# Upper halves of the weights stored with two k-tiles alternating word by word: a two-layer and two-block network on one core

## The reference

```python
def sqrelu_mlp(h, w1, w2):
    return jnp.square(jax.nn.relu(h @ w1)) @ w2
...
        up = jnp.einsum('bsd,df->bsf', h, w_up[l])
        g, val = up[..., :D_FF], up[..., D_FF:]
        g = _causal_dwconv(g, conv_w[l], conv_b[l])
        f = jnp.einsum('bsf,fd->bsd', jax.nn.gelu(g) * val, w_down[l])
        x = _layernorm(DEEPNORM_ALPHA * x + gate2[:, None, :] * f, ln2_g[l], ln2_b[l])
```

## Time and profile before

| | |
|---|---|
| Time, median of 3 runs | 2515.74 us |
| The profiled execution's span, first to last instruction | 2512.5 us |
| Instructions in the trace | 36307 |
| TensorE matmuls busy | 99% of the span, 14058 matmuls |
| Weight loads busy | 85%, 14058 loads |
| VectorE, ScalarE, GpSimd busy | 64%, 39%, 5% |
| HBM traffic | 120 GB/s over the span |

### The profile page before, as it was taken

How to read it: one execution, slowest core, us unless ns; L and a number is a source line. 1 busy time by engine, 2 the same in 40 slices (tenths; PEclk the granted TensorE clock), 3 DMA queues, 4 the chain that set the end, 5 groups by cost and what they waited for, 6 DMA issues and landing times.

```text
span 2512.5 us, 36307 instructions
## 1 busy us (share of the span) xinstructions
PE 2491.2 (99%) x14058; PEld 2125.8 (85%) x14058; DVE 1611.4 (64%) x2551; ACT 972.5 (39%) x1483; POOL 117.9 (5%) x211
## 2 busy tenths in 40 slices
PE   8999999999999999999999999999999999999998
PEld 6888888888888888779888888898888888888887
DVE  5777667665546567766655575776667777644446
ACT  6243533131313245764332244353232454533224
POOL 0000000100000000000000000010001000000000
PEclk9999999999999999999999999999999999999999
DMA  7323314433333321002545553224546323132222
GB/s 288 120 99 110 127 50 143 159 118 110 114 110 134 110 76 51 2 1 93 199 152 169 173 192 113 101 88 172 187 158 219 135 95 110 68 101 93 100 96 97
DMA packets 83965, 303.70 MB, mean 121 GB/s; under 512 B 9200, under 2 KB 11376, under 8 KB 83568
## 3 DMA queue, kind: packets, MB, share of 16 engines
q1 hardware_dynamic: 58336, 208.92, 24.0%
q0 software_dynamic: 25488, 92.81, 10.8%
HBM read 299.60 MB, written 2.10 MB: 120 GB/s over the span
## 4 chain that ended last, share of the span: by engine, by line
PE 96%; DMA 2%; DVE 1%; issue 0%; ACT 0%; SPq 0%; POOL 0%; POOLq 0%; ACTq 0%; DVEq 0%
PE G L648 20%; PE G L650 20%; PE G L649 20%; PE G L675 5%; PE G L676 5%; PE G L677 5%; PE G L742 2%; PE G L743 2%; PE G L744 2%; PE B L1243 2%; PE G L827 1%; DMA Araw<-adaw_dram 1%; PE G L829 1%; PE G L828 1%; PE B L1219 1%; PE G L1203 1%
## 5 line engine op out<-in xcount | busy, mean ns | idle before, releaser
L1391 ACT ACTIVATE Whi<-Wraw 128x1024 fp32r<-128x1024 f32 x333 | 349.6, 1051 | 411.4 <-DMA Wraw<-wstream_dram 399.3
L2038 DVE TENSOR_TENSOR Wlo<-Wraw,Whi 128x1024 fp32r<-128x1024 f32 x333 | 406.9, 1222 | 116.4 <-ACT Whi L1391 115.2
L648 PE MATMUL G<-hs_hi,Whi 128*128 128x512 f32 x672 | 264.2, 393 | 0.0
L650 PE MATMUL G<-hs_hi,Wlo 128*128 128x512 f32 x672 | 261.6, 389 | 0.0
L649 PE MATMUL G<-hs_lo,Whi 128*128 128x512 f32 x672 | 261.5, 389 | 0.0
L2053 DVE SCALAR_TENSOR_TENSOR Araw<-Araw,CB 128x1024 f32<-128x1024 f32 x176 | 214.3, 1220 | 20.6 <-DMA Araw<-adaw_dram 20.5
L2113 DVE SCALAR_TENSOR_TENSOR X<-G,MOD,X 128x256 f32<-128x256 f32 (+1 forms) x104 | 65.2, 655 | 206.0 <-PE G L650 154.9
L594 POOL DMA_DIRECT2D Araw<-adaw_dram x176 | 93.2, 530 | 1692.4 <-DVE Araw L2053 1637.9
L648 PE MATMUL G<-h_lat_hi,Whi 128*128 128x512 f32 x424 | 165.7, 391 | 0.0
L649 PE MATMUL G<-h_lat_lo,Whi 128*128 128x512 f32 x424 | 165.1, 389 | 0.0
L650 PE MATMUL G<-h_lat_hi,Wlo 128*128 128x512 f32 x424 | 165.1, 389 | 0.0
(11 more groups left out here) (636 smaller groups left out, 6169.5 us busy)
## 6 DMA issues: line engine op xcount, KB each, us to landing
Wraw<-wstream_dram SPq DMA_DIRECT2D x333, 512.0 KB, 3.3
Araw<-adaw_dram POOLq DMA_DIRECT2D x176, 512.0 KB, 3.8
Eraw<-wstream_dram SPq DMA_DIRECT2D x22, 512.0 KB, 4.4
FIRST<-firstw_dram SPq DMA_DIRECT2D x6, 1024.0 KB, 18.7
X<-xin_dram SPq DMA_DIRECT2D x4, 768.0 KB, 7.0
X<-xin_dram SPq DMA_DIRECT2D x2, 1536.0 KB, 7.3
out_dram<-X SPq DMA_DIRECT2D x16, 128.0 KB, 1.7
ROW<-rows_dram SPq DMA_DIRECT2D x2, 768.0 KB, 6.5
```

The source lines that it names most:

```text
L648: pe.matmul(o, wh, hi[:, a:b], start=(k == 0), stop=False)
L650: last = pe.matmul(o, wl, hi[:, a:b], start=False, stop=(k == kt - 1))
L1391: act.activation(hi, raw, ACT.Copy).then_inc(w_hi, 1)
L2038: dve.tensor_tensor(lo, raw, hi.bitcast(F32), ALU.subtract).then_inc(w_lo, 1)
```

## The change

In the upper halves (Whi, Ehi, Mhi) the columns of k-tiles 2j and 2j + 1 alternate word by word within their stretch of 256 words: column m of k-tile k lies at word 256 (k // 2) + 2 m + k % 2. ScalarE writes them so, VectorE reads them so when it subtracts, and each load of upper weights reads 128 words with a step of two. The raw and the lower halves stay as they were.

```diff
+        def hi_cols(k):
+
+            a = 2 * P * (k // 2) + k % 2
+            return slice(a, a + 2 * P - 1, 2)
+
+        def paired(hi):
+
+            return hi.rearrange("p (j m k) -> p j k m", j=KD // 2, k=2)
+
+        def in_rows(w):
+
+            return w.rearrange("p (j k m) -> p j k m", j=KD // 2, k=2)
...
                         if is_apart(t):
-                            wh, wl = [w[:, k * P:(k + 1) * P] for w in w_of(t)[1:]]
+                            wh, wl = w_of(t)[1][:, hi_cols(k)], w_of(t)[2][:, k * P:(k + 1) * P]
                         else:
-                            wh, wl = Whi[:, s, k * P:(k + 1) * P], Wlo[:, s, k * P:(k + 1) * P]
+                            wh, wl = Whi[:, s, hi_cols(k)], Wlo[:, s, k * P:(k + 1) * P]
...
-                act.activation(hi, raw, ACT.Copy).then_inc(w_hi, 1)
+                act.activation(paired(hi), in_rows(raw), ACT.Copy).then_inc(w_hi, 1)
...
-                dve.tensor_tensor(lo, raw, hi.bitcast(F32), ALU.subtract).then_inc(w_lo, 1)
+                dve.tensor_tensor(in_rows(lo), in_rows(raw), paired(hi.bitcast(F32)), ALU.subtract).then_inc(w_lo, 1)
```

More of the change, by code:

```diff
@@ L824, in full_part @@
                 hi, lo = src(k)
-                wh, wl = Whi[:, t % 4, k * P:(k + 1) * P], Wlo[:, t % 4, k * P:(k + 1) * P]
+                wh, wl = Whi[:, t % 4, hi_cols(k)], Wlo[:, t % 4, k * P:(k + 1) * P]
                 o = ps(bank or G[t % 2], a, b)
```

## The result

The changed kernel takes 2559.52 us, the median of four runs (2557.83 to 2565.7), against 2515.96 us for the kernel before in four runs beside them (2513.9 to 2516.93). The ratio is 1.018, with a 95% interval from 1.0166 to 1.0195: slower, by 44 us, where I had forecast no change. The time lies inside the range of 2490 to 2600 us, but what happened is none of the mechanisms that this range was built from.

The account below looks back on a forecast made before the run. TensorE's distance between matmuls was taken as the bound; 7808 upper loads x 0 plus 357 splits x 0 meant no change (chance 0.52): 2515.7 us, the runs' median, range 2490 to 2600 us.

Parts of the forecast that it names:

- What bounds the kernel: TensorE, busy 99% of the span: time comes or goes only by the distance from one matmul to the next.
- The splits at nothing: 357 splits each on ScalarE and VectorE: stepping two words adds 0; far end +0.77 us a split.
- My second rival: Each ScalarE and VectorE split 0.77 us longer, exposed at some nine joints between stages: 2530 us; chance 0.09.
- The loads at nothing: 7808 upper-weight loads on TensorE, now stepping two words: 0 ns each, far end +96 ns a load.
- The distance of 226.8 ns isn't made by how the load walks through memory: 512-column matmuls: a load reading one word 128 times gave the same distance, 0.23 us, so load price taken as 0.
- step zero: Line 1051's load reads one word 128 times: 183 ns, next 512-column matmul 0.23 us later, taken as like contiguous weights.
- My split of these loads: Of 7808 upper loads, 2512 were counted to 256-column matmuls and 5296 to 512-column ones.
- The load as the bound behind 256 columns: Strided loads outlast 256-column matmuls: at +96 ns +241 us, 2757 us; at +24 ns 2576 us; chance 0.16.
- The two faster rivals: Upper loads disturb the stream less, -17 us, 2499 us, chance 0.15; or not at all, 2412 us, chance 0.08.
- an excess: 512-column matmuls: distance 226.8 ns against the clock's 213.3, 13.5 ns a matmul, the most to be gained there.
- The observable that I named: Forecast wrong if upper loads or the distances ahead of them move by more than a nanosecond or so.

Follow-up runs that it names:

- the run with splits alone: Changed kernel with upper loads reading words in a row; both splits still write and read the upper half with a step of two words: 2515.58 us, ratio 1.0002.
- the same step zero: Against the changed kernel, all 7808 upper loads read one word 128 times and the splits are as before the change: 2523.44 us.

## Why the prediction was wrong

**What bounds the kernel** was right. Time went by the distances between matmuls and by nothing else; ScalarE's splits grew by 8% and TensorE never waited for them.

**The splits at nothing** was right for VectorE, whose splits stayed at 1.22 us, and slightly off for ScalarE: +83 ns of the 0.77 us that I kept as the far end. My second rival is refuted by the run with splits alone. So is, for this shape, the page that I cited for it: the Trainium skill, Vector Engine (DVE) Microarchitecture Reference, 5.2 Measured stream behaviour on trn2, would have had an operand that hops at every word pay; one of two sources stepping two words cost VectorE nothing here.

**The loads at nothing** is the step that failed, and the sentence in it is "a slower load costs nothing behind 512 columns until it has doubled, and costs its whole excess behind 256 columns". It treats load and stream as two things that meet only when one is longer than the other. The runs show it upside down for this change: with loads 5 to 7 ns longer the time grew by 3.0 ns a group behind 256 columns, 5.5 us in all, and behind 512 columns, with more than 100 ns of room, by 41 us. By the Trainium skill, TensorE: Matmul & The Clock Gate, Step-by-step: what each phase is for, the stream and the weights have read ports of their own, and loading the next weights takes no read bandwidth from the running matmul. The measurements differ, and they decide: with the same streams, groups of 512 columns took 680.8 ns on average with the loads of before and 688.7 to 700.4 with every other place or step that was tried. Whether the two contend for reads or get in each other's way otherwise, the runs don't tell.

**"The distance of 226.8 ns isn't made by how the load walks through memory"** was the inference that I drew from step zero, and it is false. It rested on one distance of 0.23 us, given to 10 ns, where the effect is 6.5 ns: 226.7 and 233.3 both read 0.23. By the raw starts, the eight such pairs at 512 columns in the trace before lie 226 to 234 ns apart, which bounds nothing to 6.5 ns. Where the same step zero was tried in the stream, it gave 228, 224 and 234 ns. A row can bound a cost only as finely as it is printed; with 7808 loads I needed a nanosecond, and said so myself at the end. My split of these loads was off too, without effect on a sum of zero: 1352 groups of 256 columns and 2552 of 512 make 2704 and 5104 upper loads, not 2512 and 5296.

The trace before held the warning. Timeline of the kernel before, in the hybrid stage, with mixa as the moving operand:

```profile
299.12 0.40 PE L675 MATMUL G<-mixa_hi,Whi 128*128 128x512 f32 x1
299.35 0.40 PE L676 MATMUL G<-mixa_lo,Whi 128*128 128x512 f32 x1
299.59 0.39 PE L677 MATMUL G<-mixa_hi,Wlo 128*128 128x512 f32 x1
299.82 0.28 PE L675 MATMUL G<-mixa_hi,Whi 128*128 128x256 f32 x1
```

From 299.12 to 299.82 it is 700 ns for a group of 512 columns with contiguous loads (698 in the raw starts), not 680. That stretches of 256 and 512 columns alternate here isn't the reason: of the other groups of line 675 that stand ahead of a 256-column stretch, all 112 take 680 ns. It goes with the moving operand. The 62 groups that stream mixa, mixb or mixc take 686 to 699 ns, wherever they stand; of the 2421 others 2308 take 682 or less. With the loads in their places the stream had two paces, and 680 was the better one. (All 62 lie in the hybrid stage, so that something else of that stage makes them slower isn't ruled out.) By the sizes in the kernel's list of tensors, if each lies right behind the one before (an estimate; no trace shows addresses), the three mix tensors begin 16 words past a multiple of 64 words, and every other operand streamed 512 columns at a time in these products begins at such a multiple. I saw two paces at 256 columns and took them for room for a gain, not as a sign that the pace at 512 could be lost.

**The rivals.** The load as the bound behind 256 columns: right as a mechanism, but at a step of four words; at two, the load pays 5 ns and the group 3. The two faster rivals (the load disturbs the stream less, or not at all) had the right pair of parties and the wrong sign: no kernel here has shown 512-column groups that hold a pace below 680 ns, which is the 13.5 ns over the clock that I called an excess. The observable that I named, upper loads or distances moving by more than a nanosecond, was the right one to look at: both did.

**What is settled and what is open.** Shown: the loss is the loads', nearly all of it lies behind 512 columns, and it needs no slower load and no step, since a shift by two words brings the same. Shown too: the pace at 512 columns goes with the addresses of the weights (the shifts) and with the moving operand (mixa, mixb and mixc before), and isn't fixed by them (the same unit at 693 and at 701 ns, the same slot at 680 and at 687), so that what ran before or runs beside counts as well. Likely, but only argued: stream and loads fall into a steady relation. When all loads are contiguous, of 128 columns and in their old places, it is the one at 680 ns, and in the kernel before they come back to it within a few groups after a wait (691, 692, then 680 ns in one place); in the changed kernel they settle at 693 or at about 700 instead. Why the address matters, whether by banks of the memory or otherwise, no run here tells. Whether stepped loads at some other base address would run at 680 was not tried, and no run moved the moving operand. No version beat the kernel before. Line 742's 256-column groups take 360 ns, 120 a matmul, and the same line's groups take 348 ns on average with all three loads two words later; if that could be had without the loss at 512 columns, it would be worth (360 - 348) x 544 = 6.5 us.

## What to carry to other kernels

When TensorE is full, how the weights of the next matmul lie in SBUF can be part of the current matmul's pace, even if the load is hidden twice over, as it was here. Before pricing a layout change at zero, measure the distance between matmuls over tens of steps in every stretch of the old trace: if the same instruction shows two paces, on two operands for instance, the better one can be lost by a change of address or step of the loads. Don't read a law out of differences of a few nanoseconds between single kernels before one pattern of addresses has been seen to hold one pace. And price per-instruction effects only from rows that resolve them: here 5.4 ns on each of 7656 matmuls were 41 us, 1.6% of the time.

## What the runs showed of the hardware that I had not expected

- Three 512-column fp32r matmuls, each with a 128-column load beside it, take 680 ns where the loads are contiguous and in their old places. With upper loads stepped, shifted by 8, 16 or 128 bytes, repeated or cut to 32 columns (and 32 result rows), the means are 689 to 700 ns. The granted clock was 0.997 or 0.998 throughout.
- In the kernel before, the pace also goes with the moving operand: 686 to 699 ns a group on mixa, mixb and mixc, 680 on nearly all others, with the same loads.
- One pattern of addresses can hold more than one pace for many microseconds: 693 and 701 ns in two kernels with the same loads and streams, 680 and 687 ns in two units of the kernel shifted by four words.
- A load of 32 columns takes 108 ns instead of 188. With two such loads of three, and 32 result rows, the 512-column stream is slower (group 680.8 to 696.9 ns) and the 256-column one faster (354.8 to 346.8 ns).
- The load's duration by step: 188 ns for one word, 193 to 195 for two in 512-column streams, 310 for four, 188 for zero.
- ScalarE writes 1024 words with a step of two in 1131 to 1134 ns instead of 1051; VectorE reads one of its sources so in the same 1222 ns.
